# Two query products per tick, the choice spread over more chunk groups, and expert numbers turned apart from gates

## The reference, cut to what matters

```python
def peer_rows(xr, w_query, sub_keys, expert_u, expert_v):
    q = (xr @ w_query).reshape(n, PEER_HEADS, 2, PEER_DHALF)          # 8 heads, 2 halves of 128
    s = jnp.einsum('nhcd,ckd->nhck', q, sub_keys)                     # 128 keys per half
    s1, i1 = lax.top_k(s[:, :, 0], 16); s2, i2 = lax.top_k(s[:, :, 1], 16)
    cand_s = s1[..., :, None] + s2[..., None, :]                      # 256 candidates per head
    top_s, top_pos = lax.top_k(cand_s, 16)
    eidx = ...                                                        # i1 * 128 + i2 of the 16 best
    gate = jax.nn.softmax(top_s, axis=-1)
    u = expert_u[eidx]                                                # 128 rows of 1024 per token
    h = jax.nn.gelu(jnp.einsum('nhkd,nd->nhk', u, xr))
    out = jnp.einsum('nhk,nhkd->nd', gate * h, expert_v[eidx])
```

## Time and profile before

| | us |
|---|---|
| median of 3 runs | 3025.03 (3024.61 to 3034.01) |
| profiled execution | 3024.4 |
| its span, first to last instruction | 3022.6 |
| PE busy | 2145.5 (71%) |
| DVE busy | 1785.6 (59%) |
| POOL busy | 1064.2 (35%) |
| ACT busy | 683.5 (23%) |
| DMA, whole span | 1025.97 MB, mean 339 GB/s |
| TensorE clock granted, mean share | 0.845 |

### The profile page before, as it was taken

How to read it: one execution, slowest core, us unless ns; L and a number is a source line. 1 busy time by engine, 2 the same in 40 slices (tenths; PEclk the granted TensorE clock), 3 DMA queues, 4 the chain that set the end, 5 groups by cost and what they waited for, 6 DMA issues and landing times. The chain is left out here.

```text
span 3022.6 us, 33166 instructions
## 1 busy us (share of the span) xinstructions
PE 2145.5 (71%) x11513; PEld 1128.9 (37%) x11513; DVE 1785.6 (59%) x4171; ACT 683.5 (23%) x1972; POOL 1064.2 (35%) x995
## 2 busy tenths in 40 slices
PE   7989896568776867685577676676857768555554
PEld 3447685325443533332225222243324435222221
DVE  3454438355885754764746847557745455955555
ACT  2222121112222211212511115221113322121111
POOL 1033122333664633333333434333342222354442
PEclk9999898779987978896789787887979879677788
DMA  4330430899989999999999999999999999899998
GB/s 156 104 140 1 163 126 1 307 388 390 409 314 396 387 411 416 373 395 409 358 393 418 404 417 400 358 419 419 388 417 418 419 382 420 306 364 420 420 420 331
DMA packets 152164, 1025.97 MB, mean 339 GB/s; under 512 B 17852, under 2 KB 19180, under 8 KB 34112
## 3 DMA queue, kind: packets, MB, share of 16 engines
q0 software_dynamic: 116416, 823.23, 67.2%
q1 hardware_dynamic: 35584, 200.62, 16.9%
HBM read 1003.34 MB, written 19.44 MB: 338 GB/s over the span
## 5 line engine op out<-in xcount | busy, mean ns | idle before, releaser
L1364 POOL DMA_INDIRECT fl_pairs<-in_peer_uv,fl_row_at x652 | 743.3, 1140 | 1206.4 <-PE fl_acc L1337 1085.4
L1337 PE MATMUL fl_acc<-fl_pairs,fl_diag 128*64 128x512 f32 x2608 | 835.9, 745 | 419.4 <-ACT fl_diag L1310 399.8
L1290 DVE CUSTOM_DVE_ANT_0 fl_pairs<-fl_pairs,fl_rows 128x1024 f32<-128x1024 f32 x652 | 790.2, 1233 | 430.7 <-DMA fl_pairs<-in_peer_uv,fl_row_at 430.0
L1337 PEld LDWEIGHTS fl_acc<-fl_pairs,fl_diag 128*64 128x64 f32 x2608 | 281.0, 161 | 821.2 <-issue 775.2
L1316 ACT ACTIVATE fl_acts<-fl_dots 128x2 f32<-128x2 f32 x384 | 78.1, 203 | 1253.4 <-DVE fl_dots L1290 1253.1
L1310 ACT ACTIVATE fl_diag<-constants_sb,fl_mix 128x64 f32<-128x64 f32 x768 | 224.4, 341 | 292.5 <-DVE fl_mix L1280 291.1
L1337 PE MATMUL fl_acc<-fl_more,fl_diag 128*64 128x512 f32 x464 | 149.5, 743 | 87.2 <-ACT fl_diag L1310 87.1
L1364 POOL DMA_INDIRECT fl_more<-in_peer_uv,fl_row_at x116 | 132.3, 1140 | 219.0 <-PE fl_acc L1337 198.9
L1290 DVE CUSTOM_DVE_ANT_0 fl_more<-fl_more,fl_rows 128x1024 f32<-128x1024 f32 x116 | 139.6, 1222 | 78.5 <-DMA fl_more<-in_peer_uv,fl_row_at 78.1
L1280 DVE TENSOR_TENSOR fl_mix<-fl_row_gate,fl_acts 128x2 f32<-128x2 f32 x384 | 74.7, 195 | 129.0 <-ACT fl_acts L1316 77.4
L1710 PE MATMUL aacc<-pc_piece,at_xT 128*128 128x512 f32 x288 | 138.9, 625 | 8.3 <-PEq L1623 8.3
(11 more groups left out here) (571 smaller groups left out, 2870.6 us busy)
## 6 DMA issues: line engine op xcount, KB each, us to landing
pc_piece<-in_kvq_by_pair SPq DMA_DIRECT2D x36, 1024.0 KB, 9.3
pc_piece<-in_query_by_head SPq DMA_DIRECT2D x32, 1024.0 KB, 9.6
pc_piece<-in_past_k SPq DMA_DIRECT2D x16, 1024.0 KB, 14.1
pc_piece<-in_past_v SPq DMA_DIRECT2D x16, 1024.0 KB, 12.4
ro_w_ring<-in_rwkv_w_rkv SPq DMA_DIRECT2D x24, 512.0 KB, 4.5
pc_piece<-in_out_by_pair SPq DMA_DIRECT2D x12, 1024.0 KB, 9.4
fl_pairs<-in_peer_uv,fl_row_at POOLq DMA_INDIRECT x652, 15.0
ft_ring<-in_query_by_head SPq DMA_DIRECT2D x8, 1024.0 KB, 5.0
```

The lines of the kernel that those rows point to most:

```text
L1290: dve.tensor_tensor_reduce(pair, pair, self.rows[:, u % 2, j, :], 1.0, 0.0, ALU.mult, ALU.add, self.dots[:, u % 2, q, j:j + 1]).then_inc(* ...
L1337: mm = pe.matmul(self.acc[j * FOLD:(j + 1) * FOLD, half, :], self.diag[:, self.summed % self.DIAGS, j, :], self.pair(g)[:, D + half * HALF ...
L1364: pool.indirect_dma_start(self.pair(g), None, self.io["peer_uv"], bass.IndirectOffsetOnAxis(ap=self.row_at[:, u % TILES, j, q:q + 1], axis ...
```

## The change

In the joint stage (`FirstTile`) two query products go into one tick, ticks 23 to 30, and the last score group to tick 31. ACT's copies follow at ticks 25 to 32. DVE takes each group of four top-16 in two ticks from tick 27, then the rest four steps a tick from tick 35, drained at tick 50 (`KNOWN`). The exponent stands at tick 51, the softmax at 52. POOL's four steps come at ticks 52, 54, 56 and 58. Some semaphores of this stage take the names of others and so share them.

The turn is split for all six tiles: the experts are written as soon as they are there (`expert_done`), without the softmax, and read back, and the gates are written and read back after that. `known` is set with the reading of the experts. Gathers wait for the experts alone, mixes for the gates. In the five later tiles the four steps stand in four ticks in a row, the first one to three ticks ahead of where the write stood, the last where the reading stood.

```diff
@@ Choice.rest
         if u > 0:
-            dve.wait_ge(*flow.turn_out.at(32 * u))
-        yield from settle(dve, dve.tensor_tensor(flow.expert[:], found[:, 0, :], found[:, 1, :], ALU.add), own)
+            dve.wait_ge(*flow.expert_out.at(16 * u))
+            dve.wait_ge(*flow.gate_out.at(16 * u))
+        dve.tensor_tensor(flow.expert[:], found[:, 0, :], found[:, 1, :], ALU.add).then_inc(*flow.expert_done.by())
@@ Flow.vector
             if q == 0:
-                dve.wait_ge(*self.turn_in.at(32 * GROUPS * (u + 1)))
+                dve.wait_ge(*self.gate_in.at(16 * GROUPS * (u + 1)))
@@ Flow.gpsimd
-        for u, out_at, in_at in self.turns:
-            if out_at == n:
-                self.turn_rows_out(pool, u)
-            if in_at == n:
-                self.turn_rows_in(pool, u)
+        for u, first in self.turns:
+            if first == n:
+                self.experts_out(pool, u)
+            if first + 1 == n:
+                self.experts_in(pool, u)
+            if first + 2 == n:
+                self.gates_out(pool, u)
+            if first + 3 == n:
+                self.gates_in(pool, u)
...
             if s == 0:
-                pool.wait_ge(*self.turn_in.at(32 * GROUPS * (u + 1)))
+                pool.wait_ge(*self.expert_in.at(16 * GROUPS * (u + 1)))
...
-    def turn_rows_out(self, pool, u):
+    def experts_out(self, pool, u):
+
+        pool.wait_ge(*self.expert_done.at(u + 1))
+        pool.dma_start(self.core.turn_at[u], self.expert[:]).then_inc(*self.expert_out.by(16))
+
+    def gates_out(self, pool, u):
 
         pool.wait_ge(*self.soft_done.at(u + 1))
-        pool.dma_start(self.core.turn_at[u], self.expert[:]).then_inc(*self.turn_out.by(16))
-        pool.dma_start(self.core.turn_gate[u], self.gate[:]).then_inc(*self.turn_out.by(16))
-
-    def turn_rows_in(self, pool, u):
-
-        pool.wait_ge(*self.turn_out.at(32 * (u + 1)))
+        pool.dma_start(self.core.turn_gate[u], self.gate[:]).then_inc(*self.gate_out.by(16))
+
+    def turned_in(self, pool, u, dst, src, signal):
         if u >= TILES:
             pool.wait_ge(*self.mix_done.at((u - TILES + 1) * TURNS))
-        for dst, src in ((self.row_at, self.core.turn_at), (self.row_gate, self.core.turn_gate)):
-            for s in range(GROUPS):
-                pool.dma_start(dst[s * FOLD:(s + 1) * FOLD, u % TILES], src[u].rearrange("(j w) (s q) -> s w j q", w=FOLD, q=TURNS)[s]).then_inc(*self.turn_in.by(16))
+        for s in range(GROUPS):
+            pool.dma_start(dst[s * FOLD:(s + 1) * FOLD, u % TILES], src[u].rearrange("(j w) (s q) -> s w j q", w=FOLD, q=TURNS)[s]).then_inc(*signal.by(16))
+
+    def experts_in(self, pool, u):
+
+        pool.wait_ge(*self.expert_out.at(16 * (u + 1)))
+        self.turned_in(pool, u, self.row_at, self.core.turn_at, self.expert_in)
         self.known = u + 1
+
+    def gates_in(self, pool, u):
+
+        pool.wait_ge(*self.gate_out.at(16 * (u + 1)))
+        self.turned_in(pool, u, self.row_gate, self.core.turn_gate, self.gate_in)
@@ FirstTile.gpsimd
-        if n == self.ticks:
-            self.flow.turn_rows_out(pool, 0)
-            self.flow.turn_rows_in(pool, 0)
+        if n == self.KNOWN + 2:
+            self.flow.experts_out(pool, 0)
+        if n == self.KNOWN + 4:
+            self.flow.experts_in(pool, 0)
+        if n == self.KNOWN + 6:
+            self.flow.gates_out(pool, 0)
+        if n == self.KNOWN + 8:
+            self.flow.gates_in(pool, 0)
@@ FirstTile.vector_steps
-        n = 30
+        n = 27
         for q in range(4):
             yield n
             dve.wait_ge(*self.s_done.at(q + 1))
             part = choice.best_of(dve, choice.scores, q)
-            for i in range(4):
-                advance(part, 6)
-                n += 1
-                if i < 3:
-                    yield n
+            advance(part, 10)
+            yield n + 1
             drain(part)
+            n += 2
         part = choice.rest(dve, 0)
-        while n < self.ticks:
+        while n < self.KNOWN:
             yield n
             advance(part, 4)
             n += 1
         yield n
         drain(part)
+        yield self.KNOWN + 2
         choice.softmax(dve, 0)
+
+    KNOWN = 50
@@ FirstTile.scalar_steps
-            yield 27 + 4 * q
+            yield 25 + 2 * q
...
-            yield 29 + 4 * q
+            yield 26 + 2 * q
...
-        yield self.ticks
+        yield self.KNOWN + 1
         choice.exponent(act, 0)
@@ FirstTile.tensor_steps
         for m in range(2 * PH):
-            yield 23 + m
+            if m % 2 == 0:
+                yield 23 + m // 2
...
-        yield 40
+        yield 31
         scores(3)
@@ experts_and_attention: the turns of tiles 1 to 5
-        (55, dict(choose=1, side=72, end=29, turn=((1, 31, 33),)))
+        (55, dict(choose=1, side=72, end=29, turn=((1, 30),)))
-        (125, dict(side=60, end=12, turn=((2, 14, 16),)))
+        (125, dict(side=60, end=12, turn=((2, 13),)))
-        (193, dict(side=50, end=9, turn=((3, 11, 13),)))
+        (193, dict(side=50, end=9, turn=((3, 10),)))
-        (258, dict(side=50, end=9, turn=((4, 11, 13),)))
+        (258, dict(side=50, end=9, turn=((4, 10),)))
-    run_flow(core, flow, 14, 316, choose=5, side=80, end=11, turn=((5, 13, 14),))
+    run_flow(core, flow, 14, 316, choose=5, side=80, end=11, turn=((5, 11),))
```

More of the change, by code:

```diff
@@ L3245, in experts_and_attention @@
     pieces = mixing_tile(core, io, flow, 2, ops, of_sample, later, [
-        (55, dict(choose=1, side=72, end=29, turn=((1, 31, 33),))), (62, {}), (82, {}), (90, {}), (91, {}), (97, {}), (98, {}), (107, {})])
+        (55, dict(choose=1, side=72, end=29, turn=((1, 30),))), (62, {}), (82, {}), (90, {}), (91, {}), (97, {}), (98, {}), (107, {})])
     with ExitStack() as prompt:
@@ L3250, in experts_and_attention @@
         attention_tile(core, io, flow, pieces, 0, neg_lam, kT, v_tok, [
-            (110, dict(choose=2, side=15)), (112, dict(side=15)), (125, dict(side=60, end=12, turn=((2, 14, 16),))), (131, {}), (132, {}),
+            (110, dict(choose=2, side=15)), (112, dict(side=15)), (125, dict(side=60, end=12, turn=((2, 13),))), (131, {}), (132, {}),
             (143, {}), (148, {}), (155, {}), (158, {}), (171, {})])
         attention_tile(core, io, flow, pieces, 1, neg_lam, kT, v_tok, [
-            (175, dict(choose=3, side=20)), (178, dict(side=20)), (193, dict(side=50, end=9, turn=((3, 11, 13),))), (200, {}),
+            (175, dict(choose=3, side=20)), (178, dict(side=20)), (193, dict(side=50, end=9, turn=((3, 10),))), (200, {}),
             (211, {}), (216, {}), (223, {}), (226, {}), (239, {})])
     attention_tile(core, io, flow, pieces, 2, neg_lam, None, None, [
-        (243, dict(choose=4, side=20)), (245, dict(side=20)), (258, dict(side=50, end=9, turn=((4, 11, 13),))), (263, {}),
+        (243, dict(choose=4, side=20)), (245, dict(side=20)), (258, dict(side=50, end=9, turn=((4, 10),))), (263, {}),
         (287, {}), (291, {}), (295, {}), (297, {}), (306, {})])
-    run_flow(core, flow, 14, 316, choose=5, side=80, end=11, turn=((5, 13, 14),))
+    run_flow(core, flow, 14, 316, choose=5, side=80, end=11, turn=((5, 11),))
     ffn_norm(core, io, flow, 3, 319)
```

8 lines of the change are left out of this document (4 added, 4 removed).

## The result

The changed kernel is **slower: 3043.44 us** (median of 7 runs, 3040.67 to 3049.01) against 3032.31 for the kernel before beside it (7 runs, 3024.61 to 3039.56), ratio 1.0049 with a 95% interval of 1.0035 to 1.0063. The profiled execution takes 3041.7 us with a span of 3039.9, so 17.3 more than the one before. The two medians are 11.1 us apart; the ratio with its interval says 15 (11 to 19). The forecast was 3018.8, range 3006 to 3032: wrong, and on the other side. Part of the distance of 24.6 us lies in neither kernel: the forecast started from the median of three runs, 3025.03, and the seven runs have 3032.31. As a change, -6.2 was forecast and +11 to +15 measured.

The account below looks back on a forecast made before the run. Compute bounds the kernel up to about 540 us, then a queue of DMA bytes whose start moves the end. Gathers 8.1 us earlier and 2.5 lost at later turns give -5.6 on 3024.4: 3018.8 us, range 3006 to 3032.

Parts of the forecast that it names:

- Query products, two per tick: Joint stage, PE: fourth chunk group grows from 24.9 to 36.5 us, next begins at 438.9; late weight pieces costed at nothing.
- Choice over more chunk groups: Joint stage, DVE: top-16 spread out, the rest begun at tick 35; expert numbers at 508.0 us against 522.55.
- The lock: Shared DVE and POOL port: an instruction beside a POOL instruction waits in full; by it the sum would be some 3 us lower.
- What remains behind it: Joint stage after the expert numbers: two chunk groups and the softmax; last state copy ends at 534.3 us, 3 later than before.
- Start of the gathers: End of joint stage: POOL issues row copies, then the first gather at 537.1 us against 545.17, 8.1 earlier.
- Experts apart from gates: Turns of the five later tiles: POOL waits twice and its queue can run dry; cost 2.5 us in all, range -2 to 14.
- pieces fill part: Third and fourth tiles: SP's weight pieces partly fill dry periods of 3 to 4 us; price 0 to 4 per tile.
- the tiles of 0 to 1: The later tiles other than the third and fourth, where the split turn was priced at 0 to 1 us each.
- Rival (d): Later tiles: POOL's second wait drains its queue, seven holes of 3.4 us, 24 in all; 3040 us; chance 0.12.
- (a): Joint stage: DVE packs tightly, copy ends at 526, gather 16 us earlier, turns free; 3008 us; chance 0.23.
- (b): Joint stage ends as late as now, 8 us more than summed, copy at 542; 3025 to 3027 us; chance 0.14.
- (c): Gathers start earlier but compute-bound stretches such as 600 to 620 us swallow the gain; 3024 us; chance 0.09.

Follow-up runs that it names:

- the joint stage alone: Changed kernel's first-tile joint stage with the old turn (both writes, then one wait) in the five later tiles; ratios to the kernel before 0.9982 and 0.9981.
- no_cover: Changed kernel's joint stage, one turn and one wait per later tile, no gather between writes and wait; ratio to the kernel before 1.0083.
- act_again: Changed kernel's joint stage, all turn writes and reads together on ACT's queue, POOL waiting for none; second run, another chip; ratio to the kernel before 0.9973.

## Why the prediction was wrong, point by point

- **Query products, two per tick.** Forecast 36.5 us for the fourth chunk group and a start of the next at 438.9; measured 437.44 - 400.06 = 37.4 and 437.44. The last query products end at 448.73, forecast near 448. Right, the pieces were never late: from 400 to 450 no wait of PE ended with a transfer.
- **Choice over more chunk groups.** Forecast 508.0 for the expert numbers, measured 507.17. Right, but the reason for it only in part. The digit instruction fell from 0.675 to 0.22 us and the first wide compare from 3.01 to 2.29, where POOL now stands still; at the front of the rest, which now lies beside POOL's expansions, the first wide addition rose from 2.28 to 3.12 and the cast ahead of it from 0.28 to 0.71. So 2.0 us of excess went (1.08 to 0.22 at the second digit instruction included) and 1.3 us came at another place. The lock that the prediction takes from the Trainium skill, "SBUF — State Buffer", section "SBUF: two separate sides", has a condition there that it leaves out: of DVE's instructions only those in a two-port mode take part, and those with two SBUF inputs against a GpSimd instruction that reads SBUF. No run here tests the condition.
- **What remains behind it.** Forecast 534.3 for the end of the last state copy, measured 532.37: right by the mechanism, 1.9 us too late. The granted clock was 0.86 in 495 to 520 against 0.77 before, and in the last group, 526 to 532, 0.66 against 0.77; what that cost was not separated.
- **Start of the gathers.** Forecast 537.1 for the first gather, measured 535.60, right. But the term of -8.1 in the sum was the wrong quantity: it is the gather's shift, and the queue of bytes starts with the row copies ahead of it. By the prediction's own numbers these moved from 539.18 to 534.6, so the sum should have held -4.6; measured are -6.0 at the copies, -5.9 at the first dot product, and -5.5 to -5.8 over the whole time in the two runs with that part alone. The 3.83 us of POOL's wait in the earlier trace rows looked like lost time and were cover for 1 MB of rows. That the copies fill those us is read from the rows (share 0.95 from 541 to 545 of before) and was not tested by itself.
- **Experts apart from gates: the step that failed.** The sum took 2.5 us (range -2 to 14). Measured are 23 us from the first dot product to the last in the trace, 20 between the changed kernel and the joint stage alone by the ratios, and 15 to 16 by the missing bytes of the four tiles that can be counted. The mechanism was written down: no gather between write and wait in the third and fourth tiles, the queue dry twice, waits of 5 to 10 us at the second (measured 6.86 in the third tile and 7.04 in the fourth), short dips. Two sizes were off, and perhaps a third. First, "pieces fill part": they fill nearly nothing, the share went to 0.14 (and to 0.00 in no_cover), since SP's ring is as empty as POOL's; a dry period measured 2.5 to 4.2 us, so two of them are 6 to 8 and not 0 to 4 (missing bytes: 7.0 and 7.5). Second, the second tile was put among the tiles of 0 to 1; there the gates' write has no gather behind it either, and its step is 5.3, of which 2.0 to 3.9 also stand in the kernels with the old turn; by bytes 7.7 are missing against 5.3 before (the 3.4 of the prediction were only the part of that hole from 900 to 905). Third, the sixth tile took 2.3, which is less than two executions differ by.
- **Rival (d)** put the same mechanism at seven holes of 3.4 us, 24 in all, against 23 measured. The mechanism is the one found; that the sums agree so well is partly luck, since it put 3.4 each on the second, fifth and sixth tile, where the steps are 5.3, 1.5 and 2.3 and in the fifth no bytes are missing. Its chance of 0.12 was too small because SP's pieces were held against it. The full DMA share in the third tile of before was the ground, and it was no evidence: those microseconds had POOL's own gathers still queued, so they said nothing of what SP could carry alone.

```profile
1345.00:1365.00 20.00, 15.46 (x38) 5.98 (x36) 7.15 (x15) 2.24 (x9) 6.09 (x7) 0.91 1.01 410
```

- By the Trainium skill, "DMA: Bandwidth & Descriptors", section "Queues, rings and completion order", each engine takes turns between the queues that have work. The prediction drew from it that a dry queue costs nothing while SP's has pieces. The traces do not contradict the rule; the condition was not met, since SP's queue had no work in the hole (share 0.00 at 1368 in no_cover, no piece issued between 1353.51 and 1365.90 in the changed kernel).
- Rivals (a), (b) and (c) are out: the start moved by 6, not 16 or 0, and the kernels with that part alone keep it to the end.

Open is the rest of the price of no_cover: its ratio lies 0.0101, some 30 us, above the joint stage alone, its five steps sum to 22.3 against 2.6 and 6.4 for the two joint traces, its missing bytes to 24.1 against 6.3 and 7.4. So 16 to 20 us are in the turns, and 10 to 14 are not located. Part of them can't be in this trace: the profiled execution, 3041.50 us, is the fastest of six that go up to 3058.92, and their median is 6.2 above it. What the slower ones lose no trace shows.

## What to carry to other kernels

Where a queue of gathers is the bound, count for each wait of the engine that issues them how many transfers are queued behind the one it waits for: in the third to fifth tiles two gathers (some 5 us of bytes) made both waits free, none made each cost 2.5 to 5 us. Two are enough only if the next gather is issued before their bytes run out: in the second tile of before it came when both had landed, and 5.3 us were lost. Giving the small transfers with a wait to an engine and a queue that the bound doesn't hang on left no hole at any of the four turns; in time it was ahead of the joint stage alone by 7 us on one chip and by 2 on another, where the intervals overlap. And forecast the start of a byte-bound stretch by the first large transfer of its queue, not by the first one that somebody waits for.

## What the runs showed of the hardware

- A write of 64 KB behind POOL's gathers lands late: the two kinds of write landed after 14.3 and 15.8 us in the median of before, and in no_cover POOL stood 27.77 us for one, against 1.9 and 1.8 us in the first tile of before, where no gather is queued. On ACT's queue the same writes landed after 8.3 and 11.7 us (act_again): sooner, but still far above the 1.5 and 1.6 us of the first tile there.

```profile
turn_at<-fl_expert POOLq DMA_DIRECT2D x6, 64.0 KB, 14.3
turn_gate<-fl_gate POOLq DMA_DIRECT2D x6, 64.0 KB, 15.8
```
```profile
turn_at<-fl_expert ACTq DMA_DIRECT2D x6, 64.0 KB, 8.3
turn_gate<-fl_gate ACTq DMA_DIRECT2D x6, 64.0 KB, 11.7
```

The first fence is the list of DMA issues of the kernel before, the second that of act_again: operation, count, size, median from issue to landing.
- A wide DVE instruction (128x2048) took 2.28 to 2.29 us with POOL standing still and 3.01 to 3.12 beside POOL's tensor instructions in the joint stage, and POOL's instruction was slowed as well: 3.09 us against 1.04 to 1.09 for its neighbours. The rows are from the changed kernel's DVE and POOL and from DVE of the kernel before.

```profile
463.79 3.12 DVE L1137 TENSOR_TENSOR ch_scores<-ch_best 128x2048 f32<-128x2048 f32 x1
464.73 3.09 POOL L2608 TENSOR_TENSOR hc_K_by_chunk_1w<-ops_first,constants_sb 128x512 f32<-128x512 f32 x1
481.75 2.28 DVE L1137 TENSOR_TENSOR ch_scores<-ch_best 128x2048 f32<-128x2048 f32 x1
```
